# Six tiles of the first mixing gate in Strassen's form, with its sums moved to GpSimd

## What is computed

```python
xn = rmsnorm(x, ln_g)
proj = xn @ w_in            # 1024 -> q, k, v, z_a, x_b, z_b, g_a, g_b
ret  = retention(rope(q), rope(k), v, S0)              # 4 heads, 256 x 512 states
o_a  = group_norm(ret, gn_g) * silu(z_a)
h    = rglru(causal_conv(x_b), h0)                     # width 1536, a scan over time
o_b  = h * silu(z_b)
merged = sigmoid(g_a) * (o_a @ w_a) + sigmoid(g_b) * (o_b @ w_b)
x = x + merged @ w_o
```

## Time and profile before

| | |
|---|---|
| median of 3 runs | 1893.27 us |
| profiled execution, span | 1889.0 us |
| TensorE busy | 1872.9 us (99%) |
| VectorE busy | 1306.7 us (69%) |
| ScalarE busy | 827.0 us (44%) |
| GpSimd busy | 298.6 us (16%) |

### The profile page before, as it was taken

The page is one execution under the profiler, slowest core; times in us unless marked ns, Lnnn a source line. Parts: engine busy times, 40 slices in busy tenths (PEclk is TensorE's granted clock), DMA queues, the critical chain, the costliest instruction groups (busy, mean ns, idle before and its releaser), DMA issues.

```text
span 1889.0 us, 32627 instructions
## 1 busy us (share of the span) xinstructions
PE 1872.9 (99%) x13004; PEld 1755.0 (93%) x13004; DVE 1306.7 (69%) x2260; ACT 827.0 (44%) x1352; POOL 298.6 (16%) x417
## 2 busy tenths in 40 slices
PE   9999999999999999999999999999999999999998
PEld 8899898898899999999998988988988999999997
DVE  7775665665766877866797656657557678878575
ACT  5432322423436776543444324234124377766334
POOL 2220120120231210100132201202102422001010
PEclk9999999999999999999999999999999999999999
DMA  6444534553443333543655445534444534337253
GB/s 220 137 129 159 179 132 130 163 180 110 150 147 96 104 99 99 155 134 105 199 175 162 148 124 170 178 110 152 168 119 146 167 97 107 96 93 183 90 167 116
DMA packets 119958, 264.06 MB, mean 140 GB/s; under 512 B 12510, under 2 KB 52942, under 8 KB 119678
## 3 DMA queue, kind: packets, MB, share of 16 engines
q1 hardware_dynamic: 87950, 159.94, 27.3%
q0 software_dynamic: 31712, 102.04, 17.5%
q10 hardware_dynamic: 144, 0.00, 0.0%
HBM read 203.11 MB, written 49.12 MB: 134 GB/s over the span
## 4 chain that ended last, share of the span: by engine, by line
PE 87%; DVE 5%; ACT 3%; DMA 2%; DVEq 1%; issue 1%; ACTq 1%; SPq 0%
PE bank L2414 19%; PE bank L2416 19%; PE bank L2415 19%; PE bank L2508 4%; PE bank L2509 4%; PE bank L2510 4%; PE bank L2778 2%; PE bank L2781 2%; PE bank L2780 2%; DMA w_raw<-in_w_units 2%; PE sums L2526 2%; PE sums L2508 1%; PE sums L2510 1%; PE sums L2509 1%; PE sums L2641 1%
## 5 line engine op out<-in xcount | busy, mean ns | idle before, releaser
L2414 PE MATMUL bank<-xn_hi,w_hi 128*128 128x296 f32 (+1 forms) x2016 | 603.5, 299 | 1.1 <-DVEq L2324 0.5
L2416 PE MATMUL bank<-xn_lo,w_hi 128*128 128x296 f32 (+1 forms) x2016 | 598.9, 297 | 0.0
L2415 PE MATMUL bank<-xn_hi,w_lo 128*128 128x296 f32 (+1 forms) x2016 | 598.1, 297 | 0.0
L2414 PEld LDWEIGHTS bank<-xn_hi,w_hi 128*128 128x128 f32 x2016 | 379.0, 188 | 8.4 <-issue 6.0
L671 ACT ACTIVATE w_hi<-w_raw 128x1024 fp32r<-128x1024 f32 x219 | 230.2, 1055 | 349.0 <-DMA w_raw<-in_w_units 346.4
L2415 PEld LDWEIGHTS bank<-xn_hi,w_lo 128*128 128x128 f32 x2016 | 379.5, 188 | 0.9
L2416 PEld LDWEIGHTS bank<-xn_lo,w_hi 128*128 128x128 f32 x2016 | 378.6, 188 | 0.0
L681 DVE TENSOR_TENSOR w_lo<-w_raw,w_hi 128x1024 fp32r<-128x1024 f32 x219 | 268.4, 1229 | 59.1 <-ACT w_hi L671 52.5
L2414 PE MATMUL bank<-oa_hi,w_hi 128*128 128x296 f32 (+1 forms) x512 | 153.7, 300 | 0.0
L2415 PE MATMUL bank<-oa_hi,w_lo 128*128 128x296 f32 (+1 forms) x512 | 151.9, 297 | 0.0
L2416 PE MATMUL bank<-oa_lo,w_hi 128*128 128x296 f32 (+1 forms) x512 | 151.7, 296 | 0.0
(11 more groups left out here) (347 smaller groups left out, 3846.1 us busy)
## 6 DMA issues: line engine op xcount, KB each, us to landing
w_raw<-in_w_units SPq DMA_DIRECT2D x189, 512.0 KB, 3.7
w_raw<-in_w_units SPq DMA_DIRECT2D x151, 256.0 KB, 3.4
S<-in_state_ret POOLq DMA_DIRECT2D x64, 512.0 KB, 4.8
out_ret_s<-S POOLq DMA_DIRECT2D x64, 512.0 KB, 6.2
w_raw<-in_w_units POOLq DMA_DIRECT2D x20, 256.0 KB, 4.9
vst<-v_scr SPq DMA_DIRECT2D x8, 512.0 KB, 4.1
out_ret_p<-Sp POOLq DMA_DIRECT2D x8, 512.0 KB, 5.9
v_scr<-vtok_hi SPq DMA_DIRECT2D x16, 160.0 KB
```

The lines of the kernel that those rows point to most:

```text
L2414: pe.matmul(ps, w_hi[:, slot, cols], x_hi, start=first, stop=False)
L2415: pe.matmul(ps, w_lo[:, slot, cols], x_hi, start=False, stop=False)
L2416: return pe.matmul(ps, w_hi[:, slot, cols], x_lo, start=False, stop=last)
```

## The change

Six of the eight tiles of the first gate, three pairs a layer, go through the same block form as the second gate (`GATE_ALONE = 2` tiles stay plain, `TILE_PAIRS` is 7 in place of 4). The four token sums are computed by GpSimd in heads 1 and 2, two k-blocks in each, sent to a scratch tensor in HBM and loaded again when L has ended. Three of their four low halves, and the weight sums S2 and S4, are made by GpSimd in place of VectorE. The decays of the last group go into the first two pairs, its square roots behind the second, its scans into the second and third iterations of VectorE's loop; the gate products are spread over the first four. The outputs of the branch come behind the weight sums of the fourth pair in GpSimd's queue. A gate tile of the first gate is multiplied in one operation of 592 columns in place of two. The core of the diff:

```diff
-TILE_PAIRS = KT // 2
+GATE_ALONE = 2
+FIRST_PAIRS = (KT - GATE_ALONE) // 2
+TILE_PAIRS = FIRST_PAIRS + KT // 2
+SUM_K = ((), (0, 1), (2, 3), ())
...
+                    def token_sums(k):
...
+                        def send(plane, tile):
+                            pool.drain()
+                            pool.dma_start(sum_scr[plane, :, k * HALF:k * HALF + wide], tile).then_inc(sums_out, 16)
...
+                        pool.tensor_tensor(one, hi(k, a1, b1), lo(k, a1, b1), ADD)
+                        pool.tensor_tensor(two, hi(k, a0, b0), lo(k, a0, b0), ADD)
+                        pool.tensor_tensor(four, hi(k + 4, a1, b1), lo(k + 4, a1, b1), ADD)
+                        pool.drain()
+                        pool.tensor_tensor(three, two, one, SUB)
+                        send(0, three)
+                        pool.tensor_tensor(two, one, two, SUB)
+                        pool.tensor_tensor(one, four, one, SUB)
+                        send(2, one)
+                        pool.tensor_tensor(two, two, four, SUB)
+                        pool.tensor_tensor(four, three, four, ADD)
+                        send(1, two)
+                        pool.tensor_tensor(four, four, hi(k + 4, a0, b0), SUB)
+                        pool.drain()
+                        pool.tensor_tensor(four, four, lo(k + 4, a0, b0), SUB)
+                        send(3, four)
...
                     for n in range(S_RING):
                         load_state(n)
+                    if h and l:
+                        for n in range(4):
+                            pool.wait_ge(again_in[n], 48 * (l - 1) + 16)
+                    for k in SUM_K[h]:
+                        token_sums(k)
...
+                def sum_low(count, lo, raw, hi):
+                    pool.wait_ge(right_hi, l * RIGHT_HIGHS + count)
+                    pool.tensor_tensor(lo[:, :, 0:wide], raw[:, :, 0:wide], hi[:, :, 0:wide].bitcast(f32), SUB)\
+                        .then_inc(right_lo, 1)
+
+                def add_raw(two, part, other):
+
+                    n, m = two * PRODUCTS + part, two * PRODUCTS + other
+                    wait_part(pool, l, n)
+                    if other == S1:
+                        pool.wait_ge(s1_in[two % 2], 16 * pairs_like(l, two))
+                    pool.tensor_tensor(part_of(w_raw, l, n), part_of(w_raw, l, n), part_of(w_raw, l, m), ADD)\
+                        .then_inc(part_sum, 1)
+                    pool.drain()
...
-                for two in range(TILE_PAIRS):
+                add_part(0, S1)
+                add_raw(0, S2, S1)
+                pool.wait_ge(sums_out, (l + 1) * 4 * 64)
+                wait_job(pool, "L", l, 1, ("apart", 1, 2, 1, 1))
+                load_sum(0, diff)
+                load_sum(1, mix2)
+                load_sum(2, edge)
+                load_sum(3, last_raw)
+                sum_low(1, diff_lo, diff, diff_hi)
+                add_raw(0, S4, S2)
+                add_part(0, S3)
+                sum_low(2, mix2_lo, mix2, mix2_hi)
+                sum_low(3, edge_lo, edge, edge_hi)
+                for two in range(1, TILE_PAIRS):
                     add_part(two, S1)
+                    add_raw(two, S2, S1)
                     add_part(two, S3)
+                    add_raw(two, S4, S2)
+                    if two == FIRST_PAIRS:
+                        leave_branch()
```

ScalarE's loop over the pairs (`powers(t)` is the exponential and tanh of one tile, `roots()` the three square roots, `sum_high` the copy of a loaded plane):

```diff
+                    keep_sum(two, A11, x, 0)
+                    if two == 0:
+                        part_high(two, S3)
+                        sum_high(3, xn_hi[:, 0:4, a1:b1], last_raw)
+                        keep_sum(two, S1, bank[2], 1)
+                    else:
+                        keep_sum(two, S1, bank[2], 1)
+                        part_high(two, S3)
+                    keep_sum(two, S2, x, 2)
                     part_high(two, S4)
                     part_high(two, A22)
+                    if two == 0:
+                        powers(0)
+                        powers(1)
+                    elif two == 1:
+                        powers(2)
+                    if two == FIRST_PAIRS:
+                        act.wait_ge(ob_ready, l * LT + LT)
+                        act.wait_ge(ga_used, l * KT + KT)
...
+                    if two == 1:
+                        roots()
```

VectorE's loop (`decays` are the three products of L1984):

```diff
                     part_low(two, S3)
+                    if two == 0:
+                        dve.wait_ge(right_hi, l * RIGHT_HIGHS + GATE_SUMS)
+                        dve.tensor_tensor(xn_lo[:, 0:4, a1:b1], last_raw[:, :, 0:wide], xn_hi[:, 0:4, a1:b1].bitcast(f32),
+                                          SUB).then_inc(last_ready, 1)
                     part_low(two, S4)
+                    if two == 0:
+                        gated(1)
+                    elif two == 1:
+                        decays(1, 1)
+                        gated(2)
+                    elif two == 2:
+                        scan(1, 1, 1)
+                    elif two == 3:
+                        gated(6)
+                        gated(7)
+                    dve.drain()
+                    both_sums(two, A12, bank[3], 0, c11_ready, 0, a0, b0)
                     part_low(two, A22)
+                    both_sums(two, S3, x, 1, c22_ready, 1, a1, b1)
...
+                    if two == 1:
+                        gated(3)
+                        scan(1, 1, 0)
+                    elif two == 2:
+                        gated(4)
+                        gated(5)
+                        scan(1, 1, 2)
```

340 lines of the change are left out of this document (173 added, 167 removed).

## The result

The changed kernel takes 1941.49 us (median of four runs, 1938.91 to 1941.84) against 1893.08 us of the kernel before on the same chip (1891.61 to 1893.54): a ratio of 1.0249, 95% interval 1.0235 to 1.0264. It is slower by 48 us; forecast were 16, and the range ended at 1918. The profiled execution spans 1939.6 us, 50.6 more than that of before.

A forecast was written before the change was run, and what follows sets the result against it. TensorE was taken to bound the kernel, busy 1872.9 of 1889.0 us. Stalls of 27.2 us, less 9.7 and 1.9, plus 0.5, gave +16.1 on the 1893.27 median: 1909 us, bounds 1899 and 1921, 8-in-10 range 1888 to 1918.

The forecast's parts named there:

- the 9.7 us saved: First gate, both layers: three pairs per layer in block form need 36 fewer matmuls, saving 9.7 us.
- the holes of pairs 1 and 2: TensorE waits on VectorE's PSUM sum at A22 and ScalarE's kept sum at S2: 3.4 and 4.0 us a layer.
- pair 3: Four gate products and the last scan on VectorE take 12.5 us for 11.4: stall 1.3 us a layer.
- all at full granted clock: First gate before the change: matmuls start 0.136 and 0.133 us apart, the pitch used for the saving.
- Pair 0: Token-sum planes and parts arrive late, so product S3 starts at 746.7, due at 745.7: stall 1.6 us a layer.
- GpSimd can load the token sums only when TensorE has left the branch (725.8): Start of pair 0's chain: first transfer lands after 4.4 us, the last after 7.6.
- The hold: GpSimd's weight sums block VectorE: ceiling 2x1.27 us a pair, about a third taken, in pairs 0, 2 and 3 alone.
- rival C: Weight sums and low halves on GpSimd hold VectorE for their whole length: 1918 to 1921 us; chance 0.15.
- The order on VectorE: In pairs, A22 waits behind VectorE's queued work; 1.6 us of extra work behind S4's subtraction fits, not more.
- Pair 4: Branch outputs on GpSimd wait for the last scan, ahead of this pair's S1: stall 2.3 us a layer.
- Rival A: Stalls in the pairs are absorbed because parts are ready a pair ahead: 1886 us; chance 0.17.
- Rival D: GpSimd's token sums delay splits and rotations in heads 1 and 2: 8 us on top; chance 0.05.

The follow-up runs named there:

- h1: Kernel before, with semaphore increments idling TensorE between first-gate tiles: three times 40 in layer 0, one hole of 120 in layer 1; 1926.87 us, ratio 1.0188.
- h4: Kernel before, with three idle holes in TensorE's queue per layer, 26 increments each in layer 0 and 32 in layer 1; 1909.86 us, one execution.
- e1: Changed kernel with the four token-sum loads put ahead of the first weight sum on GpSimd's queue; 1941.19 us, ratio 1.0255.
- e2: Changed kernel with ScalarE's tanhs that free the plain tiles' banks put ahead of the rounding of the token-sum planes; 1942.34 us, ratio 1.0272.
- e10: Changed kernel with the drain behind GpSimd's first weight sum moved down to just ahead of the second; 1939.79 us, ratio 1.0253.
- e9: e1 with the low parts of three token-sum planes made by VectorE in place of GpSimd; 1932.10 us, ratio 1.0215.
- f2: f1 with the planes' low parts on VectorE too, ScalarE freeing banks ahead of the third plane and its powers re-placed; 1897.25 us, ratio 1.0029.
- f1: Changed kernel with weight sums on VectorE, combined with the moves of e7 and e4; 1909.19 us, ratio 1.0098.
- h2: Changed kernel with weight sums on VectorE (1919.4 us), plus GpSimd additions nobody reads in pairs 1 to 6; 1930.07 us, ratio 1.0207.
- e7: Changed kernel with powers and decays back beside the plain tiles, roots behind pair 0, scans at the ends of pairs 0 to 2; 1928.27 us, ratio 1.0197.
- e4: Changed kernel with the branch's three outgoing transfers moved from ahead of pair 4's first weight load to behind the last pair; 1933.72 us, ratio 1.0226.
- f4: f2 with roots in the middle of pair 0, scans whole at pair ends and gate products out of their way; 1897.30 us, ratio 1.0021.
- f3: f2 with roots in the middle of pair 0 and each scan cut in two; 1903.50 us, ratio 1.0055.

## Why the prediction was wrong

Right was the sign, the 9.7 us saved, that the heads hide the token sums, and where the holes of pairs 1 and 2 stand. The holes, added up by pair, against the prediction's terms:

| pair | forecast (bounds) | layer 0 | layer 1 |
|---|---|---|---|
| 0 | 1.6 (1.2 to 2.5) | 6.0 | 7.8 |
| 1 | 3.4 (2.8 to 3.6) | 2.4 | 3.0 |
| 2 | 4.0 (2.3 to 5.4) | 5.0 | 5.8 |
| 3 | 1.3 (1.0 to 2.0) | 0 | 0 |
| 4 | 2.3 (1.0 to 3.0) | 3.2 | 4.1 |
| 5 and 6 | 1.0 (0.4 to 1.6) | 1.2 | 2.1 |
| sum | 13.6 | 17.8 | 22.8 |

The miss of 34.5 us between the spans' +50.6 and the forecast's +16.1 is, in the prediction's terms: 13.0 us of matmuls at the lower clock, for which there was no term; 10.6 us of holes in pair 0, mis-sized; 2.8 us of holes in the other pairs; 6.6 us of late starts at full clock, beyond the allowance for those of before; 1.3 us outside the two stages. Only three of the twelve figures of the pairs lie inside their bounds. That pairs 1 to 6 sum to 11.8 and 15.0 us, for 12.0 forecast, is in part luck: pair 3 had none, the others more.

1. **The clock had no term.** Matmuls at the 1.2 GHz level, none of them there before, are 13.0 us, the largest single part of the miss. The prediction read "all at full granted clock" in the earlier trace rows and carried the pitch over into a stage with holes. h1 and h4 show the mechanism in the kernel before itself. The Trainium skill, "TensorE: Matmul & The Clock Gate", section "HAM oscillation — how this bites in real kernels", describes a kernel that keeps falling back to the lower clock because it waits for data between bursts of matmuls; the traces here agree, with holes of 2.5 and 3.7 us.

2. **Pair 0 was mis-sized**, 1.6 for 6.0 and 7.8 us. The step "GpSimd can load the token sums only when TensorE has left the branch (725.8)" took the queue as free from then on; a drain held it for 6.63 us. (Its own steps, 1.3 and 0.85 us behind 735.8, end at 738.0 and not at 739.5; by them the stall forecast would have been smaller still.) The prediction followed planes and parts to S2 and S3, and never asked what ScalarE does with the banks of the plain tiles that A11 needs. e1, e2 and e10 show that neither is worth anything alone, since GpSimd's work there is serial. What paid was taking the work from it: 9 us for the planes' low parts (e9 against e1), and 12 together with ScalarE's order (f2).

3. **The hold was taken at about a third, and is whole.** The earlier trace rows had the sign of it: 2.04 us where 0.77 is usual. The ceiling of it, rival C, rested on one operation being held once, 1.27 us. The runs show more: 2.76 us beside 2.68, 6.36 beside 5.71. It was priced for weight sums only, the planes' 1184-column subtractions being the worse (f1 to f2: 12 us, with ScalarE's order in it); for sums in pairs 1 to 6 h2 gives 6.7 us, drains and late loads in it. The Trainium skill, "SBUF — State Buffer", section "Who interferes with whom", states the exclusion for the whole instruction; the trace agrees, and f1 adds that it can go on over the next instruction. C gave 1918 to 1921, still 20 us short, because it too lacked the clock and the drain.

4. **The order on VectorE was right in kind.** The holes at A22 of pairs 1 and 2 are released by its PSUM sum, one at S2 of pair 2 by ScalarE's kept sum, as forecast; A11 of pair 1 wasn't late, and pair 3 had no hole. That pairs 0 to 2 were so late that the others caught up would explain both; no run tests it. e7 and e4 price the order. e4's 7.8 us (6.0 chip by chip) are more than the 4.6 forecast for pair 4 in both layers, because slow matmuls went with the holes; e7's 13 us are less than the 17.4 forecast for pairs 1 to 3, since holes on GpSimd's chain and at the roots took the place of some. Pair 4 was low: 3.2 and 4.1 us, with 3.0 as its bound.

5. **Rival A** (absorbed, 1886) asked for an idle VectorE to run ahead. With all GpSimd arithmetic of the stage taken away f2 and f4 came within 4 to 5 us of before, so the direction of its argument was sound. But in these two the weight sums are back on VectorE, and it is full: in f2 it goes from S3's low part of pair 1 (759.45) to that of pair 2 (772.42) in 13.0 us with 0.7 of idle time, where TensorE's pair takes 11.4. f3 and f4 only move its holes. **Rival D**, 8 us in the heads, is refuted: the stretches ahead of the first stage and between the two, which hold the heads, grew by 0.8 us each.

Not settled: what the GpSimd drain waits for; how h2's 6.7 us in pairs 1 to 6 part into hold, drains and late loads; and what beside a hole's length decides whether slow matmuls follow it.
